# A hybrid decoder step on one core: products of the first norm ahead of the gates, state decay on another engine, row sums in a batch

## The chip, the cores and the metric

The kernel runs on one core of one Trainium2 chip. The metric is the device time in microseconds of one execution, the median of several runs; lower is better. In the profile the engines are PE (TensorE matmul), PEld (TensorE weight load), DVE (VectorE), ACT (ScalarE), POOL (GpSimd) and SP (SyncE, which issues the loads). `L782` is line 782 of the kernel that was profiled.

## The reference, cut to what matters

One decoder layer for 256 prompt tokens and 8 sample tokens (T = 264 columns in all), in float32, and a final norm. What the change touches is the start of the layer, up to the end of the DeltaNet branch, and the modulated norms:

```python
mod = c @ w_ada + b_ada                       # 6 vectors of 1024 per condition row
h = rmsnorm(x, norm_w) * (1 + sc) + sh        # three such norms: first, before the experts, final
qkv, z, b, a, ... = split(h @ w_in)
q, k, v = silu(short_conv(qkv))
q, k = l2norm(q) * DK ** -0.5, l2norm(k)      # 8 heads of 128 each
beta, g = sigmoid(b), -exp(A_log) * softplus(a + dt_bias)
# prompt: delta rule in chunks with a triangular solve per chunk and head
# samples: S = S * exp(g); vn = beta * (v - k S); S = S + k vn; o = q S
```

After it come the latent attention branch, the gates and the output projection, and a mixture of 32 experts (1024 by 2048 and 1024 by 1024 each). `S` are the samples' 64 states (8 heads by 8 samples) of 128 by 128 values.

## The kernel before, in words

Everything is laid out with features on the 128 partitions and tokens along the free axis. Each engine has its own hand-written program; their order is fixed by semaphores. SP streams 2 MB weight chunks in a fixed order through a ring of six slots, and refills a slot when TensorE has read the chunk in it. The stages, in order of time:

1. ACT squares x, TensorE sums the squares, and TensorE multiplies the four first chunks of `w_ada` with c (`modulate`, L731); ACT copies each result row (`mod_rows`, L1331), TensorE turns it (`turn_mod`, L737) and DVE adds the bias (`mod_bias`, L1610).
2. First norm. `norm_mod` on DVE forms 1 + scale (L1589), the reciprocal of the root (L1592) and eight products x times reciprocal (L1594), one for each of eight 128-row blocks; ACT applies scale and shift to the 256 prompt columns of each block (`modulate_prompt`, L1320); TensorE's `small_projection` (L761, L764) follows block by block.
3. The q/k/v projection: 24 output blocks m of 8 matmuls each (L782), with the short convolution on DVE and SiLU on ACT and DVE behind it. For the 16 q and k blocks ACT also squares the result (L1361, two buffers `sqb`), and TensorE sums the squares over the partitions with a four-column weight (L789): the result of block i goes to four rows at partition 32 * (i % 4) of bank 5.
4. Six more `w_ada` chunks (L731 again), then the roots and the spreading of the q/k norms over the partitions (`spread`, L813; DVE multiplies, L1661), the decays' sums (L823, L824), and copies of them in `cumc` (L1680).
5. For each of two chunks c of 128 tokens: gate rows by broadcast weights (L838 from `g_tok`, L841 from `beta_tok`), products of k with k and q (L847, L850), three more `w_ada` chunks, then the inverse of the triangular matrix by doubling in levels `lv` of 0 to 6. In each level DVE masks and updates (L1760, L1747, L1748), TensorE multiplies (L883), and ACT copies the first product (L1415, one for each of two groups g). L919 is the first matmul behind the inverse.
6. POOL, meanwhile, multiplies the samples' states, which SP loads in two 2 MB chunks (`SSM`), with their decays `egB` (L2009).
7. The samples' states, the attention branch, the gates, the output projection, the second norm, the router.
8. One pass for each of the 32 experts, whose 12.6 MB of weights go through the same ring.
9. The final norm: as stage 2, with the result stored by one DMA.

What decides the order inside a level is this code on ACT, which waits for TensorE's product of group g and copies it for TensorE's next product:

```python
for lv in range(1, LEVELS):
    for g in range(2):
        act.wait_ge(stage("lx_done"), (c * LEVELS + lv) * 2 + g + 1)
        if lv < LEVELS - 1:
            A(LTc[:, g, :], bank[g][:, 0:G2], ACT.Copy).then_inc(stage("lx_copied"), 1)
```

## Time and profile before

| what | value |
| --- | --- |
| three runs | 1711.02, 1712.14 (median), 1716.13 us |
| profiled execution, its own time | 1711.98 us |
| its span in the trace | 1710.1 us |
| PE busy / PEld busy | 1576.0 us (92%) / 850.6 us (50%) |
| DVE / ACT / POOL busy | 498.7 / 319.3 / 23.3 us |
| granted TensorE clock, mean | 0.967 of full speed |
| chain that ended last | PE 69%, DMA 14%, DVE 10%, issue 3%, ACT 2% |
| the four costliest lines in that chain | L508 14%, L551 13%, DMA of `biases` 13% (all experts), L1162 8% |

The span runs from the first to the last instruction of the program; 1.9 us of the device time lie outside it. A row of the timeline gives a group of equal instructions: start, duration from the first start to the last end, how many, and in brackets how long the engine had been idle before it and what it waited for. TensorE's float32 matmuls stand as two records each, so `x16` of L782 are eight matmuls. Bytes and GB/s are decimal; KB of a DMA are 1024 bytes.

### The profile page before, as it was taken

The numbers are of one execution on the slowest core, as the hardware profiler recorded it, in microseconds if no ns is written. First come the engines' busy times: TensorE is split into PE (matmuls) and PEld (weight loads), VectorE is DVE, ScalarE is ACT, GpSimd is POOL, SyncE is SP. The second block draws the span as 40 slices with busy tenths as digits, with TensorE's granted clock in tenths as the row PEclk, the third lists the DMA queues.
The fourth block names the chain that finished last, engine by engine and source line by source line (L and its number), as shares of the span: only waits on it lengthen the run. The fifth ranks groups of instructions, "written<-read, shape, count | busy, mean of one in ns | idle before, by whom it ended". The sixth has DMA issues, their size and how long they took to land.

```text
span 1710.1 us, 25650 instructions
## 1 busy us (share of the span) xinstructions
PE 1576.0 (92%) x10122; PEld 850.6 (50%) x10122; DVE 498.7 (29%) x1073; ACT 319.3 (19%) x688; POOL 23.3 (1%) x17
## 2 busy tenths in 40 slices
PE   5998687998879999789999999999999999999996
PEld 3777676576547768433333434333333334333332
DVE  1455765623210102422222222222222222222223
ACT  2222121112321110211111112111111112111113
POOL 0000300000000000000000000000000000000000
PEclk8998799999979999879999999999999999999999
DMA  9638502534238996249999999999999999999990
GB/s 403 272 110 333 208 30 121 209 124 164 72 105 304 346 343 264 94 190 405 428 427 425 428 427 427 429 428 428 429 429 427 427 423 428 420 428 423 429 420 34
DMA packets 59534, 541.25 MB, mean 317 GB/s; under 512 B 7218, under 2 KB 11442, under 8 KB 28626
## 3 DMA queue, kind: packets, MB, share of 16 engines
q1 hardware_dynamic: 58754, 534.65, 76.0%
q0 software_dynamic: 720, 5.76, 0.8%
q8 instruction: 43, 0.70, 0.2%
q14 instruction: 17, 0.14, 0.0%
HBM read 533.54 MB, written 6.84 MB: 316 GB/s over the span
## 4 chain that ended last, share of the span: by engine, by line
PE 69%; DMA 14%; DVE 10%; issue 3%; ACT 2%; SPq 1%; POOL 0%; DVEq 0%; ACTq 0%
PE banks L508 14%; PE banks L551 13%; DMA regC<-biases 13%; PE banks L1162 8%; PE banks L782 5%; PE banks L491 2%; PE banks L539 2%; DVE regA L629 2%; PE banks L521 2%; PE banks L1036 2%; PE banks L478 2%; PE banks L980 2%; DMA ring<-wpre 1%; DVE regA L627 1%; DVE regA L626 1%
## 5 line engine op out<-in xcount | busy, mean ns | idle before, releaser
L508 PE MATMUL banks<-ring,regA 128*64 128x512 f32 x2048 | 454.5, 596 | 0.8 <-ACT regA L566 0.8
L508 PEld LDWEIGHTS banks<-ring,regA 128*64 128x64 f32 x2048 | 144.7, 137 | 287.6 <-issue 287.6
L551 PE MATMUL banks<-ring,regC 128*64 128x512 f32 x1024 | 226.8, 595 | 0.0
L604 DVE TENSOR_TENSOR regB<-regB,banks 128x528 f32<-128x528 f32 x132 | 84.0, 699 | 383.7 <-PE banks L491 383.7
L551 PEld LDWEIGHTS banks<-ring,regC 128*64 128x64 f32 x1024 | 70.7, 137 | 131.8 <-issue 127.9
L624 DVE TENSOR_SCALAR regA<-banks 128x512 f32<-128x512 f32 x32 | 22.1, 691 | 339.4 <-PE banks L521 339.4
L569 ACT ACTIVATE regA<-regA 128x512 f32<-128x512 f32 x32 | 20.1, 630 | 517.3 <-DVE regA L624 517.3
L464 PE MATMUL banks<-regC,regA 128*64 128x512 f32 (+1 forms) x396 | 99.7, 621 | 3.3 <-DVE regA L596 3.3
L782 PE MATMUL banks<-hT,ring 128*128 128x264 f32 x384 | 90.3, 391 | 0.0
L782 PEld LDWEIGHTS banks<-hT,ring 128*128 128x128 f32 x384 | 71.5, 190 | 18.3 <-issue 7.0
L491 PE MATMUL banks<-regA,regC 64*128 64x264 f32 x528 | 73.8, 409 | 0.7 <-ACT regC L581 0.7
L491 PEld LDWEIGHTS banks<-regA,regC 64*128 64x128 f32 x528 | 45.4, 186 | 42.3 <-issue 26.0
L1162 PE MATMUL banks<-hT,ring 128*128 128x264 f32 x256 | 57.9, 387 | 0.0
L581 ACT ACTIVATE regC<-banks 128x512 f32<-128x512 f32 x32 | 19.1, 597 | 205.8 <-PE banks L551 205.8
L883 PE MATMUL banks<-regC 64*64 64x64 f32 x960 | 36.1, 235 | 19.8 <-DVE regC L1760 19.8
L1162 PEld LDWEIGHTS banks<-hT,ring 128*128 128x128 f32 x256 | 48.3, 190 | 10.0 <-issue 1.1
L539 PE MATMUL banks<-con_sb,regA 128*128 128x128 f32 x256 | 37.1, 288 | 17.3 <-DVE regA L629 17.3
L464 PEld LDWEIGHTS banks<-regC,regA 128*64 128x64 f32 (+1 forms) x396 | 22.8, 136 | 50.5 <-issue 50.5
L883 PEld LDWEIGHTS banks<-regC 64*64 64x64 f32 x960 | 33.4, 149 | 22.5 <-DVE regC L1760 22.5
L731 PE MATMUL banks<-ring,small_sb 128*32 128x128 f32 x1024 | 33.0, 282 | 9.4 <-DMA ring<-wpre 5.7
L569 ACT ACT_TABLE_LOAD x32 | 41.1, 1283 | 0.6
L539 PEld LDWEIGHTS banks<-con_sb,regA 128*128 128x128 f32 x256 | 31.0, 191 | 20.2 <-DVE regA L629 20.2
(445 smaller groups left out, 1646.6 us busy)
## 6 DMA issues: line engine op xcount, KB each, us to landing
ring<-w_gu SPq DMA_DIRECT2D x128, 2048.0 KB, 16.3
ring<-w_dn SPq DMA_DIRECT2D x64, 2048.0 KB, 13.9
ring<-wpre SPq DMA_DIRECT2D x41, 2048.0 KB, 13.7
ring<-kvT SPq DMA_DIRECT2D x64, 256.0 KB, 4.8
ring<-kv SPq DMA_DIRECT2D x64, 256.0 KB, 6.2
ring<-ssm SPq DMA_DIRECT2D x2, 2048.0 KB, 10.6
o_ssms<-ring POOLq DMA_DIRECT2D x2, 2048.0 KB, 7.4
con_sb<-con SPq DMA_DIRECT2D x1, 1269.0 KB
```

The lines of the kernel that those rows point to most:

```text
L464: mm = pe_mm(bank[2][SLOT * y:SLOT * (y + 1), :], lhsT=self_[r, i, :], rhs=h2tok[r, i, 4 * y:4 * y + 4, :].rearrange("p k c -> p (k c)"), ...
L478: mm = pe_mm(bank[3][:, P * q:P * (q + 1)], lhsT=gtok[:, P * q:P * (q + 1)], rhs=ident, start=True, stop=True)
L491: mm = pe_mm(bank[b + y][:, 0:T], lhsT=ytok[r, P * q:P * (q + 1)], rhs=selT[r, :], start=True, stop=True)
L508: mm = pe_mm(bank[x // 2][SLOT * (x % 2):SLOT * (x % 2 + 1), :], lhsT=hg[:, k % 4, SLOT * (k // 4):SLOT * (k // 4 + 1)], rhs=ring[c][:, 20 ...
L521: mm = pe_mm(bank[u][SLOT * y:SLOT * (y + 1), :], lhsT=ones[32 * u:32 * u + 1, 0:SLOT], rhs=brow[32 * u:32 * u + 1, HALF * y:HALF * (y + 1 ...
L539: mm = pe_mm(bank[4 - 2 * y][:, P * q:P * (q + 1)], lhsT=act_[:, P * q:P * (q + 1)], rhs=ident, start=True, stop=True)
L551: mm = pe_mm(bank[5][SLOT * y:SLOT * (y + 1), :], lhsT=actT[:, m % 4, SLOT * (m // 4):SLOT * (m // 4 + 1)], rhs=ring[c][:, D * (m % 4) + H ...
L569: A(sgm[:, :], gmn[:, :], ACT.Sigmoid, scale=1.702).then_inc(sig_ready, 1)
L604: V.tensor_tensor(pair, pair, banks[:, b:b + 2, 0:T], ALU.add).then_inc(acc_added, 1)
L782: mm = pe_mm(bank[m % 4][:, 0:T], lhsT=chunk_k(n, m % 4, k), rhs=hT[:, k, :], start=(k == 0), stop=(k == KD - 1))
L883: mm = pe_mm(out[rows, s], lhsT=left[rows, s], rhs=right(i, rows, cols), start=True, stop=True)
L1162: mm = pe_mm(bank[4 + m % 2][:, 0:T], lhsT=chunk_k(n, m % 4, k), rhs=rhs[:, k, :], start=(k == 0), stop=(k == KD - 1))
```

## The change

It has five parts.

- **First norm.** `norm_mod` is split in three. `normalised` (reciprocal and eight products) is now called ahead of the four `mod_bias` of the first chunks; `norm_scale` and `modulate_rest` come behind them. In all three norms ACT modulates the first five blocks (`ACT_K`), and DVE the other three with `tensor_scalar`.
- **Row sums.** The 16 row-sum matmuls of the q and k blocks leave the projection loop and are issued as one batch behind it. `sqb` grows from 2 buffers to 16 and moves to another place in the same memory.
- **Banks.** `spread` uses banks 0 to 3 in place of 4, 5, 0, 1.
- **Gate rows.** TensorE's wait for the last of the 16 q/k norms (`l2done`) moves from ahead of the gate rows of chunk 0 to behind them.
- **State decay.** POOL's two instructions over 128 x 4096 values are gone. ACT does the same in 64 instructions over 128 x 128 values with a per-partition scale, seven of them ahead of each level's copies: levels 3 to 6 of chunk 0 and 1 to 6 of chunk 1 (one in the last).

The diff (constants and buffers; TensorE; ACT; DVE; POOL):

```diff
@@ -43,10 +43,14 @@
 NJ1 = NJ + 1
 LEVELS = 7
 MOD_PRE = 10
-L2_BANKS = (4, 5, 0, 1)
+L2_BANKS = (0, 1, 2, 3)
 VALUE_BANKS = (2, 3, 0, 1)
 MOD_L2 = 7
 MOD_GDN = 3
+DECAY_FROM = 2
+DECAY_STEP = 7
+ACT_K = 5
+NORM_STEPS = 1 + 2 * KD - ACT_K
 
 
 C_ID, C_ONE, C_EPS = 0, 128, 256
@@ -156,7 +160,7 @@
 
         upad = cut(regC, 0, 3, 3 + NPR)
         sigb = cut(regC, 800, 2, T)
-        sqb = cut(regC, 1400, 2, T)
+        sqb = cut(regC, 3500, 2 * H, NPR)
         sq_s = cut(regC, 1400, 2 * H, NSA)
         rsb = cut(regC, 2900, 2, T)
         modA = cut(regC, 2300, KD, 9)
@@ -757,7 +761,10 @@
             def small_projection(out, weights_of, r):
 
                 for k in range(KD):
-                    pe.wait_ge(stage("modulated"), r * KD + k + 1)
+                    if k < ACT_K:
+                        pe.wait_ge(stage("modulated"), r * ACT_K + k + 1)
+                    else:
+                        pe.wait_ge(stage("normed"), r * NORM_STEPS + 1 + KD + k - ACT_K + 1)
                     pe_mm(out[:, 0:NPR], lhsT=weights_of(k), rhs=hT[:, k, 0:NPR], start=(k == 0), stop=(k == KD - 1), skip_group_check=True)
                 pe.wait_ge(h_ready, r + 1)
                 for k in range(KD):
@@ -783,13 +790,11 @@
                                start=(k == 0), stop=(k == KD - 1))
                 mm.then_inc(proj_ready, 1)
 
-                i = m - 3
-                if 0 <= i < 2 * H:
-                    pe.wait_ge(l2sq, i + 1)
-                    pe_mm(group_sum(i, slice(0, NPR)), lhsT=row_sum(i // 4, 4), rhs=sqb[:, i % 2, 0:NPR], start=(i < 4), stop=(i >= 2 * H - 4),
-                          skip_group_check=True).then_inc(l2ss, 1)
-
-
+            pe.wait_ge(l2sq, 2 * H)
+            for i in range(2 * H):
+                mm = pe_mm(group_sum(i, slice(0, NPR)), lhsT=row_sum(i // 4, 4), rhs=sqb[:, i, :], start=(i < 4), stop=(i >= 2 * H - 4),
+                           skip_group_check=True)
+            mm.then_inc(l2ss, 1)
             pe.wait_ge(proj_evac, CONVT)
             for i in range(4, MOD_PRE + 1):
                 if i < MOD_PRE:
@@ -815,8 +820,10 @@
 
             pe.wait_ge(stage("l2_rs"), 1)
             for i in range(2 * H):
+                if i == 0:
+                    pe.wait_ge(mod_row, MOD_PRE)
                 if i == 2:
-                    pe.wait_ge(mod_row, MOD_PRE)
+                    pe.wait_ge(mod_evac, MOD_PRE)
                 if i == 2 * H - 4:
                     pe.wait_ge(bg_done, 1)
                     for c in range(2):
...
@@ -825,7 +832,6 @@
                     pe.wait_ge(stage("bgm_ready"), 1)
                     pe_mm(bank[6][:, 96:160], lhsT=ones[0:NSA, :], rhs=bgm[0:NSA, :], start=True, stop=True).then_inc(once("cum_ready")[0], 1)
                 spread(i)
-            pe.wait_ge(l2done, 2 * H)
 
             for c in range(2):
                 tok = slice(c * P, (c + 1) * P)
@@ -842,6 +848,7 @@
                     if g == 0 and c == 0:
                         pe.wait_ge(*once("cum_read"))
                         pe.wait_ge(stage("egB_ready"), 1)
+                        pe.wait_ge(l2done, 2 * H)
                     for i in range(4):
                         h = 4 * g + i
...
@@ -1315,8 +1322,8 @@
 
             def modulate_prompt(r, out, sh, A9):
 
-                for k in range(KD):
-                    act.wait_ge(stage("normed"), r * KD + k + 1)
+                for k in range(ACT_K):
+                    act.wait_ge(stage("normed"), r * NORM_STEPS + 1 + (KD if r == 0 else k + 1))
                     A(out[:, k, 0:NPR], out[:, k, 0:NPR], ACT.Identity, scale=A9[:, k, 0:1], bias=mod[:, sh + k, 0:1]).then_inc(stage("modulated"), 1)
 
             def root(out, sums, scale):
@@ -1356,9 +1363,7 @@
                 i = m - 2
                 if 0 <= i < 2 * H:
                     act.wait_ge(silu_done, i + 1)
-                    if i >= 2:
-                        act.wait_ge(l2ss, i - 1)
-                    A(sqb[:, i % 2, 0:NPR], qkvT[:, i, 0:NPR], ACT.Square).then_inc(l2sq, 1)
+                    A(sqb[:, i, :], qkvT[:, i, 0:NPR], ACT.Square).then_inc(l2sq, 1)
             for i in range(4, 6):
                 mod_rows(i, i % 2)
             act.wait_ge(stage("conv_s"), 1)
@@ -1369,18 +1374,29 @@
             A(beta_tok[:, :, :], gsc[:, 0, :, :], ACT.Sigmoid).then_inc(ab_act, 1)
 
             act.wait_ge(silu_done, CONVT + 1)
-            act.wait_ge(l2ss, 2 * H)
             A(sq_s[:, :, :], qkvT[:, 0:2 * H, NPR:T], ACT.Square).then_inc(l2sq, 1)
             for i in range(6, MOD_PRE):
                 mod_rows(i, i % 2)
                 if i == MOD_L2:
-                    act.wait_ge(l2ss, 2 * H + 1)
+                    act.wait_ge(l2ss, 2)
                     A(rsb[:, 0, :], bank[5][:, 0:T], ACT.Sqrt, scale=1.0, bias=con[:, C_EPS:C_EPS + 1]).then_inc(root_ready, 1)
 
             link(A(gsc[:, 2, :, :], gsc[:, 1, :, :], ACT.Abs))
             link(A(gsc[:, 2, :, :], gsc[:, 2, :, :], ACT.Exp, scale=-1.0))
             link(A(gcol[:, 0, :], small[:, S_ALOG:S_ALOG + 8], ACT.Exp))
             A(gsc[:, 2, :, :], gsc[:, 2, :, :], ACT.Ln, bias=1.0).then_inc(ab_act, 1)
+
+            def decay(first):
+
+                for i in range(first, min(first + DECAY_STEP, H * NSA)):
+                    g, r = i // 32, i % 32
+                    if r == 0:
+                        act.wait_ge(stage("egB_ready"), 1)
+                        act.wait_ge(slot_in[(SSM + g) % RING], arrive[SSM + g])
+                    S = ssm_view[g][:, r // NSA, r % NSA, :]
+                    ins = A(S, S, ACT.Copy, scale=egB[:, i:i + 1])
+                    if r == 31:
+                        ins.then_inc(stage("decayed"), 1)
 
             for c in range(2):
 
@@ -1409,6 +1425,8 @@
                 for i in range(MOD_GDN):
                     mod_rows(MOD_PRE + MOD_GDN * c + i, 4 + i % 2)
                 for lv in range(1, LEVELS):
+                    if c == 1 or lv > DECAY_FROM:
+                        decay(DECAY_STEP * ((LEVELS - 1 - DECAY_FROM if c else 0) + lv - (1 if c else DECAY_FROM + 1)))
                     for g in range(2):
                         act.wait_ge(stage("lx_done"), (c * LEVELS + lv) * 2 + g + 1)
                         if lv < LEVELS - 1:
...
@@ -1584,20 +1602,34 @@
                 ins.then_inc(dve_line, 1)
                 dve.wait_ge(dve_line, line[0])
 
-            def norm_mod(r, x, out, sc, sh, nw, rs, A9):
-
-                link(V.scalar_tensor_tensor(A9, mod[:, sc:sc + KD, :], 1.0,
-                                            small[:, nw:nw + KD].unsqueeze(2).to_broadcast([P, KD, 9]), ALU.add, ALU.mult))
+            def normalised(r, x, out, rs):
+
                 dve.wait_ge(root_ready, (1, 6, 7)[r])
                 link(V.reciprocal(rs, rs))
                 for k in range(KD):
                     V.tensor_tensor(out[:, k, :], x[:, k, :], rs, ALU.mult).then_inc(stage("normed"), 1)
 
-                dve.wait_ge(stage("normed"), (r + 1) * KD)
+            def norm_scale(sc, nw, A9):
+
+                V.scalar_tensor_tensor(A9, mod[:, sc:sc + KD, :], 1.0, small[:, nw:nw + KD].unsqueeze(2).to_broadcast([P, KD, 9]),
+                                       ALU.add, ALU.mult).then_inc(stage("normed"), 1)
+
+            def modulate_rest(r, out, sh, A9):
+
+                dve.wait_ge(stage("normed"), r * NORM_STEPS + 1 + KD)
+                for k in range(ACT_K, KD):
+                    V.tensor_scalar(out[:, k, 0:NPR], out[:, k, 0:NPR], A9[:, k, 0:1], mod[:, sh + k, 0:1], ALU.mult, ALU.add).then_inc(stage("normed"), 1)
                 link(V.tensor_tensor(out[:, :, NPR:T], out[:, :, NPR:T], A9[:, :, 1:9], ALU.mult))
-                dve.wait_ge(stage("modulated"), (r + 1) * KD)
+                dve.wait_ge(stage("normed"), (r + 1) * NORM_STEPS)
+                dve.wait_ge(stage("modulated"), (r + 1) * ACT_K)
                 V.tensor_tensor(out[:, :, NPR:T], out[:, :, NPR:T], mod[:, sh:sh + KD, 1:9], ALU.add).then_inc(h_ready, 1)
                 dve.wait_ge(h_ready, r + 1)
+
+            def norm_mod(r, x, out, sc, sh, nw, rs, A9):
+
+                norm_scale(sc, nw, A9)
+                normalised(r, x, out, rs)
+                modulate_rest(r, out, sh, A9)
 
             dve.wait_ge(inputs_in, 48)
             link(V.memset(upad[:, :, 0:3], 0.0))
@@ -1610,11 +1642,13 @@
                 V.tensor_tensor(mod[:, 4 * i:4 * i + 4, :], bank[b][:, at:at + P].rearrange("p (m c) -> p m c", c=32)[:, :, 0:9],
                                 small[:, S_BADA + 4 * i:S_BADA + 4 * i + 4].unsqueeze(2).to_broadcast([P, 4, 9]),
                                 ALU.add).then_inc(mod_evac, 1)
+            dve.wait_ge(*once("upad_zero"))
+            normalised(0, xT[:, :, :], hT[:, :, :], rsb[:, 0, :])
             for i in range(4):
                 mod_bias(i, 2 + i % 2)
             dve.wait_ge(mod_evac, 4)
-            dve.wait_ge(*once("upad_zero"))
-            norm_mod(0, xT[:, :, :], hT[:, :, :], 8, 0, S_NMIX, rsb[:, 0, :], modA[:, :, :])
+            norm_scale(8, S_NMIX, modA[:, :, :])
+            modulate_rest(0, hT[:, :, :], 0, modA[:, :, :])
 
             dve.wait_ge(stage("rest_in"), 48)
             for m in range(CONVT + 1):
...
@@ -2002,11 +2036,6 @@
             pool.dma_start(t["o_convp"], convp[:, :, :]).then_inc(stored, 16)
             pool.dma_start(t["o_convs"], samp[:, :, :, :]).then_inc(stored, 16)
 
-            pool.wait_ge(stage("egB_ready"), 1)
-            for g in range(2):
-                pool.wait_ge(slot_in[(SSM + g) % RING], arrive[SSM + g])
-                S = ssm_view[g].rearrange("p h b v -> p (h b) v")
-                nc.gpsimd.tensor_tensor(S, S, egB[:, 32 * g:32 * g + 32].unsqueeze(2).to_broadcast([P, 32, P]), ALU.mult).then_inc(stage("decayed"), 1)
```

**TensorE, the projection loop (stage 3).** Before, the rows of the program from the small projection to the first later `w_ada` chunk. Names: `hT` is the normed input, `ring` a weight chunk, `regC` in L789 is `sqb`.

```order
L761 MATMUL banks<-hT,small_sb 16x256 x8
L764 MATMUL banks<-hT,small_sb 16x8 x8
L782 MATMUL banks<-hT,ring 128x264 x8
L775 MATMUL banks<-con_sb,regC 128x16 x2
L775 MATMUL banks<-con_sb,regC 8x16
L782 MATMUL banks<-hT,ring 128x264 x24
L789 MATMUL banks<-regC,con_sb 4x256
L782 MATMUL banks<-hT,ring 128x264 x8
...
L789 MATMUL banks<-regC,con_sb 4x256
L782 MATMUL banks<-hT,ring 128x264 x40
L731 MATMUL banks<-ring,small_sb 32x128 x64
```

And in the changed kernel (line numbers shift; L789 is now the projection, L795 the row sums):

```order
L768 MATMUL banks<-hT,small_sb 16x256 x8
L771 MATMUL banks<-hT,small_sb 16x8 x8
L789 MATMUL banks<-hT,ring 128x264 x8
L782 MATMUL banks<-con_sb,regC 128x16 x2
L782 MATMUL banks<-con_sb,regC 8x16
L789 MATMUL banks<-hT,ring 128x264 x184
L795 MATMUL banks<-regC,con_sb 4x256 x16
L735 MATMUL banks<-ring,small_sb 32x128 x64
```

The 16 row sums stood one behind each of the blocks 3 to 18; they now stand together behind block 23.

**DVE, the first norm (stage 2).** Before, from the last of the opening memsets to the first convolution:

```order
L1606 MEMSET banks 128x264
L1610 TENSOR_TENSOR mod<-banks,small_sb 128x36 x4
L1589 SCALAR_TENSOR_TENSOR regC<-mod,small_sb 128x72
L1592 RECIPROCAL regC<-regC 128x264
L1594 TENSOR_TENSOR hT<-xT_sb,regC 128x264 x8
L1597 TENSOR_TENSOR hT<-hT,regC 128x8x8
L1599 TENSOR_TENSOR hT<-hT,mod 128x8x8
```

In the changed kernel, the same stretch:

```order
L1638 MEMSET banks 128x264
L1608 RECIPROCAL regC<-regC 128x264
L1610 TENSOR_TENSOR hT<-xT_sb,regC 128x264 x8
L1642 TENSOR_TENSOR mod<-banks,small_sb 128x36 x4
L1614 SCALAR_TENSOR_TENSOR regC<-mod,small_sb 128x72
L1621 TENSOR_SCALAR hT<-hT,regC,mod 128x256 x3
L1622 TENSOR_TENSOR hT<-hT,regC 128x8x8
L1625 TENSOR_TENSOR hT<-hT,mod 128x8x8
```

The reciprocal and the products now stand ahead of the gates' bias, and three blocks of modulation (`TENSOR_SCALAR`) are new on DVE.

**ACT, the inverse of chunk 0 (stage 5).** Before, from the last exponential of the chunk's preparation to the output's copies:

```order
L1403 ACTIVATE regC<-regC 128x512
L1331 ACTIVATE mrow<-banks 128x128 x3
L1415 ACTIVATE regC<-banks 128x256 x10
L1417 ACTIVATE regC<-banks 64x256 x2
L1428 ACTIVATE regB<-banks 128x4x128 x2
```

In the changed kernel, behind the three copies of gate rows (L1397 is the decay, `ring` the states, L1433 and L1435 the levels' copies):

```order
L1433 ACTIVATE regC<-banks 128x256 x4
L1397 ACTIVATE ring<-ring,egB 128x128 x7
L1433 ACTIVATE regC<-banks 128x256 x2
L1397 ACTIVATE ring<-ring,egB 128x128 x7
L1433 ACTIVATE regC<-banks 128x256 x2
L1397 ACTIVATE ring<-ring,egB 128x128 x7
L1433 ACTIVATE regC<-banks 128x256 x2
L1397 ACTIVATE ring<-ring,egB 128x128 x7
L1435 ACTIVATE regC<-banks 64x256 x2
L1446 ACTIVATE regB<-banks 128x4x128 x2
```

Seven decay instructions stand ahead of the two copies of each level from the third on.

## Rows read from the trace of the kernel before

**Rows 1.** Busy time by stretch, expert stage: busy us (count) by engine, PEclk, DMA share, GB/s.
```profile
800.00:1000.00 200.00, 196.20 (x1049) 76.97 (x1046) 47.99 (x95) 32.69 (x53) 0.00 (x0) 1.00 1.01 427
```

**Rows 2.** Timeline, 10 to 45 us: start us, us, engine, line, operation, count [idle before].
```profile
15.38 0.48 ACT L1323 ACTIVATE regC<-banks,con_sb 128x264 f32<-128x264 f32 x1 [4.34 <-PE banks L717]
...
32.43 1.80 DVE L1592 RECIPROCAL regC<-regC 128x264 f32<-128x264 f32 x1
34.26 2.84 DVE L1594 TENSOR_TENSOR hT<-xT_sb,regC 128x264 f32<-128x264 f32 x8
34.73 4.04 ACT L1320 ACTIVATE hT<-hT,mod,regC 128x256 f32<-128x256 f32 x8 [3.44 <-DVE hT L1594]
...
35.38 6.16 PE L761 MATMUL banks<-hT,small_sb 128*16 128x256 f32 x16 [3.49 <-ACT hT L1320]
...
41.86 3.83 PE L782 MATMUL banks<-hT,ring 128*128 128x264 f32 x16
```

**Rows 3.** Chain that ended last, first microseconds: start us, us, what.
```profile
3.84 25.03 DMA ring<-wpre
```

**Rows 4.** DMA issues, 0 to 60 us: operation, count, KB each.
```profile
con_sb<-con SPq DMA_DIRECT2D x1, 1269.0 KB
...
regB<-convT SPq DMA_DIRECT2D x1, 384.0 KB
```

**Rows 5.** Busy time by stretch, 36 to 42 us, columns as in rows 1.
```profile
36.00:42.00 6.00, 6.00 (x32) 2.52 (x31) 1.55 (x6) 2.80 (x7) 0.00 (x0) 0.62 1.02 434
```

**Rows 6.** Timeline, end of the q/k/v projection.
```profile
117.23 3.83 PE L782 MATMUL banks<-hT,ring 128*128 128x264 f32 x16
...
121.51 18.07 PE L782 MATMUL banks<-hT,ring 128*128 128x264 f32 x80
...
140.19 3.70 PE L731 MATMUL banks<-ring,small_sb 128*32 128x128 f32 x128 [0.61 <-ACT regC L1349]
```

**Rows 7.** Timeline, 165 to 175 us: last q/k norms, then the gate rows.
```profile
168.31 1.82 DVE L1661 SCALAR_TENSOR_TENSOR regA<-regA,banks 128x264 f32<-128x264 f32 x4 [2.19 <-PE banks L813]
...
170.18 2.08 PE L838 MATMUL banks<-con_sb,g_tok 128*128 128x128 f32 x8 [1.98 <-DVE regA L1661]
...
171.01 0.19 DVE L1680 COPY cumc<-banks 128x32 f32<-128x32 f32 x1
...
173.72 1.05 PE L847 MATMUL banks<-regA 128*128 128x128 f32 x8
```

**Rows 8.** Timeline, first chunk's inverse, 195 to 232 us.
```profile
195.20 14.20 POOL L2009 TENSOR_TENSOR ring<-ring,egB 128x4096 f32<-128x4096 f32 x2 [46.91 <-DMA ring<-ssm]
...
197.90 0.42 DVE L1747 TENSOR_TENSOR regC<-regC,banks 128x256 f32<-128x256 f32 x1 [2.80 <-PE banks L883]
...
198.81 3.70 DVE L1760 TENSOR_TENSOR regC<-regC,con_sb 128x256 f32<-128x256 f32 x1
...
203.32 6.35 DVE L1760 TENSOR_TENSOR regC<-regC,con_sb 128x256 f32<-128x256 f32 x1
...
230.44 1.83 PE L919 MATMUL banks<-regC 128*128 128x128 f32 x14
```

**Rows 9.** All instructions of line 1760: ns min/median/max, first and last start.
```profile
L1760 DVE TENSOR_TENSOR regC<-regC,con_sb x24: 414/424/6352, 191.3 to 278.9; 128x256 f32<-128x256 f32 x24
```

**Rows 10.** Timeline, second chunk's inverse, 263 to 286 us.
```profile
263.86 0.42 DVE L1747 TENSOR_TENSOR regC<-regC,banks 128x256 f32<-128x256 f32 x1 [1.72 <-PE banks L883]
...
265.97 0.38 ACT L1415 ACTIVATE regC<-banks 128x256 f32<-128x256 f32 x1 [2.67 <-PE banks L883]
...
285.53 1.16 PE L919 MATMUL banks<-regC 128*128 128x128 f32 x8
```

**Rows 11.** ACT by line: names, shapes, count | busy us, mean ns | idle before us.
```profile
L1361 ACT ACTIVATE regC<-regA 128x256 f32<-128x256 f32 x16 | 6.8, 427 | 0.0
...
L1373 ACT ACTIVATE regC<-regA 128x128 f32<-128x128 f32 x1 | 0.3, 293 | 0.0
```

**Rows 12.** Timeline, last norm.
```profile
1705.47 0.23 DVE L1599 TENSOR_TENSOR regC<-regC,mod 128x64 f32<-128x64 f32 x1 [1.51 <-ACT regC L1320]
```

More of the change, by code:

```diff
@@ L1659, in _ @@
             for i in range(2 * H):
-                dve.wait_ge(l2ss, 2 * H + 2 + i)
+                dve.wait_ge(l2ss, 3 + i)
                 V.scalar_tensor_tensor(qkvT[:, i, :], qkvT[:, i, :], P ** -0.5 if i < H else 1.0, bank[L2_BANKS[i % 4]][:, 0:T], ALU.mult, ALU.mult).then_inc(l2done, 1)
```

## The prediction

> **What bounds the kernel now.** I read the chain that ended last first, then the expert stage by stretches, then the timeline of the first 300 us, where the change is. In the expert stage TensorE is busy 196.2 of 200 us and the DMA share is 1.01 at 427 GB/s [rows 1]: both are at their limit, and nothing of the change touches that stage. Its first loads are issued when TensorE releases ring slots, so it has no date of its own: whatever the start gains shifts it whole. The question is what the start gains. There TensorE waits for others, mostly DVE and ACT, so each part is read from the wait that ends last at its place.
>
> **First norm.** The root is ready at 15.86 us, while the last gate chunk lands only at 28.87 [rows 2, 3]. Before, the reciprocal (1.80) and the first product stand behind the gates: DVE starts them at 32.43, ACT follows at 34.73, TensorE at 35.38 [rows 2]. Moved ahead, reciprocal and products take 15.9 to 20.6, in the time of the weights' load; without that cover they would cost their 4.7 us again. ACT can then start at about 32.5, TensorE 0.65 later, as it does now, at 33.1: 2.3 us earlier. What is late next? The small projection takes 6.2 us, at a granted clock that stands at 0.62 over 36 to 42 us [rows 2, 5], so half clock most of that time, behind a TensorE idle of 3.49 us [rows 2]. With an idle of only 1.3 us it may keep the full clock. Then ACT's five blocks (4.04 / 8, 0.5 each) and DVE's three, which are done early, set the pace: done at about 37.2, 4.7 earlier. The next limit is the first projection chunk. Behind the last gate chunk (28.87) the queue still has 1269 KB and 384 KB [rows 4] and that chunk's 2 MB: 3.8 MB, at 434 GB/s [rows 5] 8.7 us, so it lands at 37.6 to 38, against a first use at 41.86 [rows 2]. Gain: 1.9 (clock half) to 3.9 (DMA bound); I take 3.6, since the shorter idle favours the full clock.
>
> **Row sums.** With a row sum behind it, one output block takes 121.51 - 117.23 = 4.28 us; the five without one take 18.07 together, 3.6 each, 3.56 without the tail [rows 6]. Sixteen times 0.72 is 11.5 us, and it includes TensorE's pauses around each. The loop's other engines have shown that they follow at 3.56 in those last blocks; ACT's squares go on, 0.43 each [rows 11]. The wait of 0.61 us for ACT's last copy behind the loop [rows 6] is covered by the batch. The batch itself is not in the trace. From the nearest row: the gate matmuls put four results in four groups of 32 output rows, as the row sums do; 64 matmuls of 128 columns take 3.70 us [rows 6], so 4096 columns take 1.85, and the batch has 16 x 256 = 4096. With 0.2 for the change of shape: 2.1. Upper bound, if they run one after the other as the projection's do: 3.56 / 8 x 256 / 264 = 0.43 each, 6.9. I take 2.1, because the output positions are those of the gate matmuls. Gain 11.5 + 0.6 - 2.1 = 10.0; 5.2 at the other end. The squares of the last q/k block are long there when the batch starts.
>
> The Trainium skill (TensorEngine Tiling (Array Packing), Key Properties and Theoretical Speedup) says that tiles work in parallel, up to four of them for a stationary operand of at most 32 columns, and that a change of tiling mode drains the engine. By it the batch would be 6.9 / 4 = 1.7 us, and the pauses around each row sum are such drains. No run here shows that of four-column weights yet.
>
> **Banks and gate rows.** Spreads into banks 2 and 3 now wait for the last gate bias on DVE. That is done before DVE's first two q/k norms, which need banks 0 and 1 only: nothing. The gate rows (L838, L841) used to start at 170.18, behind DVE's last norm; the products of k follow at 173.72 [rows 7], 3.54 us of TensorE. Moved ahead, they start when the last spreads are out, 168.3 [rows 7], and end at 171.85. The products also wait for the copy on DVE, done at 171.20 [rows 7], so about 171.35. Gain: 1.9, and 2.35 if the clock is full there; eight records of L838 took 2.08 against 1.05 of L847 [rows 7], so half clock. I take 1.9.
>
> **State decay.** POOL's two instructions run from 195.20 to 209.40. In just that time two of DVE's mask products (L1760, both inputs in the main memory) take 3.70 and 6.35 us [rows 8], against a median of 0.424 over 24 [rows 9], while L1747, which reads a bank, keeps its 0.42 [rows 8]. The second chunk runs the same levels with POOL idle, so it prices the whole: from L1747 of level 2 to L919 it takes 285.53 - 263.86 = 21.67 us, the first chunk 230.44 - 197.90 = 32.54 [rows 8, 10]. The difference, 10.87, is 9.2 of the two stalls and 1.7 of matmuls at a lower clock behind them. Bounds: 9.2, if the clock is low for another reason; 12, if levels 0 and 1 also run at full clock. I take 10.9.
>
> What ACT pays: 64 instructions, seven a level. In a level ACT waits 2.67 us for TensorE ahead of its first copy [rows 10]; the seven must fit in that gap. Price of one: the modulation, 256 columns with scale and bias from memory, steps at 4.04 / 8 = 0.505 [rows 2]; 128 columns fewer cost 0.427 - 0.293 = 0.134 less [rows 11]. So 0.37 at most, 7 x 0.37 = 2.6: hidden, barely. Below, 0.29 as the plain one of 128 columns [rows 11]; above, 0.505, which makes 3.5 and 0.9 us a level. The Trainium skill (ScalarE: Activation LUTs, What ACT_TABLE_LOAD costs) gives 186 ns + 0.833 ns a column and 93 ns for each operand from memory, with 93 of overlap: 0.29 a piece, 2.1 us for seven, by which half a microsecond of the gap is left. The first group needs the first state chunk; POOL's start shows that it landed at 195.20, while DVE enters level 2 only at 197.90, and the first decay stands behind that level's copies [rows 8]. I take no cost.
>
> **Last norms.** At the second norm TensorE's small projection sets the pace, not ACT: nothing. At the last, DVE's L1599 at 1705.47 waits for ACT's eighth block [rows 12]. Now ACT does five, and DVE puts three blocks in place of its wait of 1.51 us; at L1747's 0.42 [rows 8] they take 1.26: 0.25 us earlier, somewhat more with a scalar form. I take 0.3.
>
> **Sum.** 3.6 + 10.0 + 1.9 + 10.9 + 0.3 = 26.7 us. The profiled execution took 1711.98 us (1710.1 span and 1.9 around it), practically the median of 1712.14. 1711.98 - 26.7 = 1685.3 us.
>
> **Rivals.**
> - *The row sums do not run side by side* (four-column weights are handled as wide ones). Against: the same output groups as the gate matmuls. 4.8 us less: 1690.1.
> - *ACT is late in the levels.* Each decay costs 0.5 or the copies queue behind it. What stands behind a late decay is the level's first copy, and TensorE's doubling waits for that. For: the margin is thin by my own price. 0.9 x 9 levels = 8 us less: 1693.
> - *Slower than before.* Same mechanism, decisive when the decays of nine levels lose over 26.7 us, 3.0 a level: one decay of 0.81 us, (2.67 + 3.0) / 7, or 52 us of ACT in all. That is over twice the dearest price that I can derive. At 1.0 us a piece the time would be 1685.3 + 9 x 4.3 = 1724.
> - *No change.* The stalls of DVE are not POOL's doing and stay (10.9 less), and the experts' weight stream takes back the rest because its start isn't tied to the stages ahead. Against: L1760 is slow in POOL's time only, and the stream's slots are released by TensorE. 1712.
>
> **How the numbers follow.** Forecast as summed, each term within its bounds: 0.75. Row sums in series: 0.09. ACT late: 0.09. Slower: 0.02. Around no change: 0.02, and 0.03 for losses I have no name for, half of the gain or more. The best of all terms, 3.9 + 10.1 + 2.35 + 12 + 0.4, is 28.8, and full clock in the norms' stage, where those eight records cost double, may add 2 us: 1681. The other end holds the two middle rivals up to about 1692. Anything within 0.3% (5 us) is hardly told from no change; all cases but the last few lie far outside. Faster 0.95, same 0.03, slower 0.02.
>
> **What would show it.** Right: the small projection starts at about 33 us and the first projection block at about 38; all projection blocks 3.56 apart, the batch of 32 records about 2 us; the products of k start directly behind the gate rows; L1760's successor never over 0.5 us; seven decays in 2.1 to 2.6 us and TensorE's gaps in chunk 0 like those of chunk 1; the expert stage unchanged, only earlier. Wrong: a batch of 7 us, copies of a level starting after TensorE's product has long ended, TensorE waiting for a chunk at 33 to 40 us beyond 38, or a new pause of TensorE for its code or clock at 125 to 160 us.

## The result

The changed kernel takes 1703.04 us in the median of 15 runs (1683.51 to 1708.24); the kernel before, beside it, 1715.33 (1704.86 to 1732.34). The ratio is 0.9897, 95% interval 0.987 to 0.9923: faster by 1.0%. The forecast was 1685.3 with a range from 1681 to about 1692; its gain, 26.7 us, is more than twice the 12.3 us measured.

The median hides what the single times show. They lie in two groups with nothing between: six from 1683.5 to 1686.9 us, around the forecast, and nine from 1702.2 to 1708.2. The mean granted clock splits them too: 0.973 to 0.976 of full speed in the lower group, 0.961 to 0.965 in the upper. The profiled execution belongs to the lower group (1686.86 us). From its page:

```profile
span 1685.0 us, 25694 instructions
...
PE 1562.3 (93%) x10122; PEld 850.0 (50%) x10122; DVE 492.5 (29%) x1082; ACT 334.2 (20%) x743; POOL 9.0 (1%) x15
...
PEclk9998999999979999799999999999999999999998
```

Its timeline, first norm (start and duration in us, engine, line, operation, operands, shape, count, and in brackets the idle time before and what ended it):

```profile
32.26 2.58 ACT L1327 ACTIVATE hT<-hT,mod,regC 128x256 f32<-128x256 f32 x5 [1.14 <-DVE regC L1614]
...
32.92 3.87 PE L768 MATMUL banks<-hT,small_sb 128*16 128x256 f32 x16 [1.19 <-ACT hT L1327]
...
37.79 3.80 PE L789 MATMUL banks<-hT,ring 128*128 128x264 f32 x16 [0.61 <-DMA ring<-wpre]
```

TensorE starts the small projection 2.5 us earlier than in [rows 2], at full clock (3.87 us), and then waits for the first projection chunk: 4.07 us gained.

The same timeline at the projection's end, in the stage of the six `w_ada` chunks and in that of the gate rows:

```profile
123.84 1.91 PE L795 MATMUL banks<-regC,con_sb 128*4 128x256 f32 x32
125.57 3.45 PE L735 MATMUL banks<-ring,small_sb 128*32 128x128 f32 x118
130.94 0.60 PE L735 MATMUL banks<-ring,small_sb 128*32 128x128 f32 x10 [1.92 <-issue]
...
137.93 0.64 PE L735 MATMUL banks<-ring,small_sb 128*32 128x128 f32 x16 [2.22 <-issue]
...
144.69 1.73 PE L735 MATMUL banks<-ring,small_sb 128*32 128x128 f32 x54 [2.59 <-issue]
...
147.28 1.07 PE L818 MATMUL banks<-regC,con_sb 4*128 4x264 f32 x8
...
156.32 2.08 PE L844 MATMUL banks<-con_sb,g_tok 128*128 128x128 f32 x8
158.19 1.91 PE L847 MATMUL banks<-con_sb,beta_tok 128*128 128x128 f32 x8
159.90 1.40 PE L854 MATMUL banks<-regA 128*128 128x128 f32 x8
```

The kernel before, in the same stage:

```profile
148.85 0.64 PE L731 MATMUL banks<-ring,small_sb 128*32 128x128 f32 x16 [0.79 <-issue]
...
155.34 2.05 PE L731 MATMUL banks<-ring,small_sb 128*32 128x128 f32 x54 [2.32 <-issue]
...
158.54 1.26 PE L813 MATMUL banks<-regC,con_sb 4*128 4x264 f32 x8
```

The batch of row sums takes 1.91 us. The gate chunks start at 125.57 against 140.19 [rows 6], 14.62 earlier. In their stage TensorE now pauses three times with nothing to wait for ("issue"), 6.7 us in all; before it paused twice, 3.1 us. From the first gate chunk to the first spread it takes 21.71 us against 18.35, and from there to the gate rows 9.04 against 11.64. The products of k, which follow the gate rows directly, are 13.82 us earlier than in [rows 7].

And in the first chunk's inverse, with all instructions of the mask product (ns min/median/max) below:

```profile
183.35 0.42 DVE L1781 TENSOR_TENSOR regC<-regC,banks 128x256 f32<-128x256 f32 x1 [1.72 <-PE banks L890]
...
187.00 2.15 ACT L1397 ACTIVATE ring<-ring,egB 128x128 f32<-128x128 f32 x7
187.65 0.42 DVE L1781 TENSOR_TENSOR regC<-regC,banks 128x256 f32<-128x256 f32 x1 [1.72 <-PE banks L890]
...
205.04 3.63 PE L926 MATMUL banks<-regC 128*128 128x128 f32 x16
```

```profile
L1794 DVE TENSOR_TENSOR regC<-regC,con_sb x24: 416/426/426, 177.8 to 254.5; 128x256 f32<-128x256 f32 x24
```

From level 2 to the first matmul behind the inverse it is 205.04 - 183.35 = 21.69 us, against 32.54 in [rows 8] and 21.67 in [rows 10]. No mask product takes over 0.426 us; seven decays take 2.15 us and are done before DVE's update needs anything of ACT.

The span is 25.1 us shorter (1710.1 - 1685.0), 1.6 less than the sum. So in an execution of the lower group the change gains about what the prediction says. What puts most executions 17 us or more higher is the question of the experiments.

### The profile page after: what moved, and what is told of

The parts are those of the page before. It is cut to its first block and busy times, and to the rows that moved or that the text cites. A ratio compares the mean times of both kernels' runs of the same rounds, so it can differ in the third digit from the quotient of the medians.

```text
span 1685.0 us, 25694 instructions
## 1 busy us (share of the span) xinstructions
PE 1562.3 (93%) x10122; PEld 850.0 (50%) x10122; DVE 492.5 (29%) x1082; ACT 334.2 (20%) x743; POOL 9.0 (1%) x15
## 5 line engine op out<-in xcount | busy, mean ns | idle before, releaser
L789 PE MATMUL banks<-hT,ring 128*128 128x264 f32 x384 | 85.9, 386 | 0.6 <-DMA ring<-wpre 0.6
L789 PEld LDWEIGHTS banks<-hT,ring 128*128 128x128 f32 x384 | 72.8, 190 | 13.1 <-issue 0.7
L1169 PE MATMUL banks<-hT,ring 128*128 128x264 f32 x256 | 57.9, 387 | 0.0
L890 PE MATMUL banks<-regC 64*64 64x64 f32 x960 | 32.3, 220 | 11.7 <-DVE regC L1794 11.7
L525 PE MATMUL banks<-regC,con_sb 1*64 1x512 f32 x256 | 34.8, 612 | 3.9 <-DMA regC<-biases 3.9
## 6 DMA issues: line engine op xcount, KB each, us to landing
ring<-ssm SPq DMA_DIRECT2D x2, 2048.0 KB, 10.6
```

Source lines behind the costliest of these rows:

```text
L525: mm = pe_mm(bank[u][SLOT * y:SLOT * (y + 1), :], lhsT=ones[32 * u:32 * u + 1, 0:SLOT], rhs=brow[32 * u:32 * u + 1, HALF * y:HALF * (y + 1 ...
L789: mm = pe_mm(bank[m % 4][:, 0:T], lhsT=chunk_k(n, m % 4, k), rhs=hT[:, k, :], start=(k == 0), stop=(k == KD - 1))
L890: mm = pe_mm(out[rows, s], lhsT=left[rows, s], rhs=right(i, rows, cols), start=True, stop=True)
L1169: mm = pe_mm(bank[4 + m % 2][:, 0:T], lhsT=chunk_k(n, m % 4, k), rhs=rhs[:, k, :], start=(k == 0), stop=(k == KD - 1))
```

## The experiments

Each experiment ran beside the kernel before on the same chip. A kernel's times fell into two groups, called the lower and the upper level, whose medians lie 15 to 21 us apart (26 in e7, which has a single run on the upper one), unless one of the groups was empty. The kernel before has them too, but in all its 102 timed runs only 10 lie on the upper one (1727.6 to 1733.7 us; the other 92 from 1704.9 to 1720.0). Which level a run belongs to is told by its time; a profile on the upper level was taken in e8, e11 and e12, of the whole change none.

### One part at a time, and the change without one part

**The whole change again** (e1).

> The changed kernel once more, to see its two levels of time (span 1681 to 1685 at a mean granted clock of .973 to .976, and 1700 to 1706 at .961 to .965) and, if the profiled execution falls on the upper one, to find the stretch in which it lies. Theory A (a place in the program that the change moved is left at half clock longer in some executions): both levels appear again, in about 6 executions of 15 the lower, and the kernel before, on the same chip, shows one level about 1711 to 1717. Theory B (the levels belong to the chip or the moment and touch any kernel): the kernel before shows two levels 17 us apart as well, on the same chip.

Six runs: 1684.78, 1685.65, 1688.93 and 1703.26, 1705.04, 1705.57. Two levels again, 12 of 21 executions on the upper one with the first 15.

**Single parts**: POOL's instructions replaced by ACT's `decay` (e2), the row sums in one batch (e3), the first norm split (e4), each in the kernel before.

> The kernel before with the states' decay on ACT alone. The sum of the prediction gives 10.9 us (9.2 to 12), a time of about 1701 in the profiled execution. Theory A: if this part is what brings the second level, its times split 17 us apart; otherwise they stay together. Theory B: splits as every other kernel on this chip does.

> The kernel before with the q/k row sums in one batch behind the projection alone. By the prediction 10.0 us less (11.9 for what goes away from the projection's end and the rope's wait, less 2.1 for the batch), about 1702; 5.2 us of batch if the column groups ran in series, about 1705. Theory A: if this part brings the second level, its times split 17 us apart.

> The kernel before with the first norm's products split off and made during the loads, alone. By the prediction 3.6 us less (1.9 to 3.9), about 1708. Theory A: if this part brings the second level, its times split 17 us apart.

On the lower level their medians are 1701.2 (9 of 12 runs), 1704.7 (11 of 12) and 1707.2 (10 of 12), against 1713.5 for the kernel before (27 of 29). The parts can also be read from the start of the first outer product of the samples' states, behind all four: 307.72 us before, 297.13, 298.27 and 303.57 with one part, 283.33 with the whole change. That is 10.6 for the decay (sum: 10.9), 9.5 for the row sums (10.0), 4.2 for the norm (3.6), 24.4 for all (26.4 without the last norm). Each is one profile, and they scatter: in e1 the same program has that start at 286.18, 2.9 us later, with more time at half clock and pauses of 5.1 in place of 6.7 us ahead of it. So these sums are good to about 3 us. All three have the upper level, in 3, 1 and 2 of 12: no single part makes it frequent.

**Without one part** (e5 to e8).

> The whole change without its row sums in a batch. On the lower level the sum gives 1684.7 + 10.0 = 1695 us. So far single parts lie on the upper level (17 to 21 us higher) in 1 to 3 executions of 12, the kernel before in about 4 of 44, the whole change in 12 of 21. Theory A (one part of the change, or where it moves a later stretch, makes the upper level frequent): the four kernels that leave out one part each differ in their share of the upper level, and the one that lacks the guilty part falls back to 1 or 2 in 10. Theory B (no part, only the moment on the chip): all four and the kernel before show like shares. A profile of an execution on the upper level will show the stretch: by the mean granted clocks (.974 against .962) about 38 us more at the lower clock, where TensorE sets the pace.

> The whole change without the states' decay on ACT. Lower level: 1684.7 + 10.9 = 1696 us. Theory A: if the decay is the guilty part, the upper level (about 1713) comes in 1 or 2 executions of 10 here, and in half of those of the other three. Theory B: like shares.

> The whole change without the first norm's split. Lower level: 1684.7 + 3.6 = 1688 us. Theory A: if the first norm is the guilty part, the upper level (about 1706) is rare here. Theory B: like shares.

> The whole change without the gate rows and banks ahead of the last norms. Lower level: 1684.7 + 1.9 = 1687 us. Theory A: if this part is guilty, the upper level (about 1704) is rare here. Theory B: like shares.

| without | lower level | upper level |
| --- | --- | --- |
| row sums | 6 runs, 1690.6 to 1693.3 | 4 runs, 1710.7 to 1715.7 |
| decay | 7 runs, 1690.9 to 1704.6 | 3 runs, 1716.6 to 1721.7 |
| first norm | 3 runs, 1689.2 to 1689.8 | 1 run, 1715.2 |
| gate rows | 5 runs, 1687.6 to 1695.6 | 5 runs, 1706.0 to 1709.8 |

The lower levels' medians are 1691.7, 1699.7, 1689.4 and 1691.2 us, against 1695, 1696, 1688 and 1687 expected; the run without the decay spreads over 14 us. No kernel falls back to 1 or 2 in 10, so the shares name no guilty part. But the profile of the one without the gate rows was taken on the upper level (span 1704.7 us). Its windows (engine busy times, granted clock PEclk, DMA share, GB/s):

```profile
280.00:290.00 10.00, 8.15 (x46) 4.95 (x39) 8.67 (x11) 2.06 (x3) 0.00 (x0) 0.83 0.00 2
290.00:300.00 10.00, 10.00 (x21) 3.72 (x19) 2.81 (x4) 0.00 (x0) 0.00 (x0) 0.50 0.01 2
300.00:310.00 10.00, 10.00 (x20) 4.38 (x20) 3.63 (x3) 0.39 (x1) 0.54 (x1) 0.50 0.50 210
310.00:320.00 10.00, 10.00 (x29) 3.87 (x32) 3.06 (x4) 0.39 (x1) 0.53 (x1) 0.50 0.12 52
320.00:330.00 10.00, 10.00 (x58) 6.16 (x51) 6.36 (x5) 0.39 (x1) 0.00 (x0) 0.96 1.01 391
```

The whole change on the lower level, the same stretch:

```profile
280.00:290.00 10.00, 8.14 (x33) 4.12 (x33) 8.31 (x12) 0.39 (x1) 0.00 (x0) 1.00 0.00 0
290.00:300.00 10.00, 10.00 (x39) 4.50 (x38) 6.06 (x8) 0.39 (x1) 0.54 (x1) 1.00 0.50 211
300.00:310.00 10.00, 10.00 (x60) 5.72 (x59) 6.30 (x7) 0.78 (x2) 0.53 (x1) 1.00 0.82 311
```

Here is the 17 us: TensorE is at half clock (1.2 GHz) from about 287 to 321 us, 34 us, although it is busy 10.00 of 10. Its work there takes about twice as long, and TensorE sets the pace. Over 1700 us such a stretch lowers the mean clock by 0.010, about what parts the two groups of the result. The timelines at its entry, first without the gate rows, then the whole change:

```profile
280.41 3.83 PE L985 MATMUL banks<-hT,ring 128*128 128x264 f32 x16
286.09 1.63 PE L998 MATMUL banks<-regC 32*128 32x512 f32 x4 [1.85 <-DVE regC L1831]
287.65 2.13 PE L985 MATMUL banks<-hT,ring 128*128 128x264 f32 x4
289.71 2.08 PE L998 MATMUL banks<-regC 32*128 32x512 f32 x4
```

```profile
277.65 3.83 PE L987 MATMUL banks<-hT,ring 128*128 128x264 f32 x16
283.33 1.13 PE L1000 MATMUL banks<-regC 32*128 32x512 f32 x4 [1.86 <-DVE regC L1833]
284.39 1.16 PE L987 MATMUL banks<-hT,ring 128*128 128x264 f32 x4
```

The work and the idle ahead of it are the same, 1.85 and 1.86 us, and so in each profile with the idle unfilled, before the change too (1.85 to 1.88): TensorE has done the z block and waits for DVE's `vnm`, then alternates outer products, which use 32 of the 128 rows (L998 or L1000), with steps of the next z block. Only the clock differs. The theory from here on: where that idle falls between the moments at which the clock can change decides, and the change, which moves the idle by 24.4 us (21.5 in e1), has moved it to an unlucky place (theory P).

### Shifting the idle, and filling it

The pad, in the whole change or in the kernel before, behind the second chunk's inverse:

```diff
+                for k in range(3 if c == 1 else 0):        # or 6
+                    pe_mm(bank[0][:, 0:T], lhsT=ident, rhs=hT[:, k, :], start=True, stop=True)
                 for g in range(2):
                     pe.wait_ge(stage("x_done"), (c + 1) * 2 * LEVELS if g == 1 else (c + 1) * 2 * LEVELS - 1)
```

The fill, in the idle itself (`beta` moves from bank 6 to unused columns of bank 4):

```diff
             project_z(0, 0, KD)
+            for k in range(3):
+                pe_mm(bank[6][:, 0:T], lhsT=chunk_k(ZZ, 0, k), rhs=hT[:, k, :], start=True, stop=True)
             pe.wait_ge(*once("krow_copied"))
```

> The changed kernel, plus six matmul records of 264 columns into an unused bank (1.4 us, results thrown away) in TensorE's idle of 1.86 us ahead of the first outer product of the samples' states; the copy of beta moves to bank 4 for it. Theory P (in some executions that idle ends just before the clock is reviewed, TensorE then works 34 us at half clock through the samples' states, and that is the upper level): the upper level vanishes, all executions at about 1685 to 1690. Theory D (the decay on ACT brings the upper level by itself, or it lies elsewhere): the upper level stays in about half of the executions, median about 1700.

> The changed kernel, plus 1.44 us of idle work (three products of 264 columns into bank 0) behind the second chunk's inverse, about 20 us ahead of that idle; the idle itself stays. Theory P with a phase that the program's own length sets: the idle falls 1.4 us later against the clock's moments, as it does in the kernel before; the upper level is seen in about 1 of 10 executions, so the median is about 1687, below the changed kernel's 1700 although there is more work. Theory P with a random phase: the share stays about half. Theory D: the share stays about half, every time 1.4 us longer.

> The kernel before with the same 1.44 us of idle work at the same place. Theory P with a phase set by the program's length: here the shift leads into the bad place; the upper level comes in more than half of the executions, median about 1730 against 1713. Theory P with a random phase, and theory D: about 1 in 10 as before, median 1714.5.

> The changed kernel with six such products, 2.87 us. [...] Theory P with a random phase, and theory D: about half, median anywhere from 1688 to 1705, lower level 1687.

The next four kernels keep the unlucky shift and take the idle away, or fill it with the kernel's own work: with `beta` in bank 4 the second z block needn't wait for DVE any more.

```diff
             project_z(0, 0, KD)
+            project_z(1, 0, 3)
+            cuts = ((3, 5, 6, 7, 8), (0, 2, 4, 6, 8))
...
-                    project_z(1 + g, 2 * x, 2 * x + 2)
+                    project_z(1 + g, cuts[g][x], cuts[g][x + 1])
```

> The changed kernel with three of the eight steps of the second z block made in the idle ahead of the first outer product (1.44 us of its own work, no more idle work), the other five between the outer products. Theory P: no upper level; the work moved into the idle also shortens the stretch by up to 1.4 us: about 1683 to 1686 in all executions. Rival (the thin products behind the idle let the clock fall): with fewer dense steps between them the upper level stays or becomes frequent, about 1700.

> The kernel that lay on the upper level in all its executions (six products of idle work, median 1704.8), with the idle filled by thrown-away products. Theory P: all executions back on the lower level, 1685.9 + 2.9 = about 1688.5. Rival (thin products): stays at 1704.

> The kernel before with three pad products (median 1729.3, all on the upper level), with the idle filled. Theory P: back to about 1713. Rival: stays at 1729.

> The six pad products with the idle filled by the second z block's own steps. Theory P: 1704.8 falls to about 1687, all executions together. Rival: some executions stay 17 us higher, since fewer dense steps lie between the thin products.

| kernel | median us | runs on the upper level | ratio to before, 95% |
| --- | --- | --- | --- |
| before | 1711.1 to 1715.3 | 10 of 102 | 1 |
| before, shifted 1.4 us (e11) | 1729.3 | 6 of 6 | 1.0104 (1.0082 to 1.0126) |
| the same, idle filled (e15) | 1714.5 | 0 of 12 | 1.0003 (0.9976 to 1.0029) |
| whole change | 1703.0, 1696.1 | 12 of 21 | 0.9897 (0.987 to 0.9923) |
| shifted 1.4 us (e10) | 1688.35 | 1 of 6 | 0.9877 (0.9839 to 0.9915) |
| shifted 2.9 us (e12) | 1704.8 | 10 of 10 | 0.9959 (0.9942 to 0.9976) |
| the same, idle filled (e14) | 1691.7 | 0 of 6 | 0.9878 (0.9841 to 0.9915) |
| the same, own work in the idle (e16) | 1689.7 | 0 of 6 | 0.9858 (0.9822 to 0.9895) |
| whole change, idle filled (e9) | 1685.94 | 0 of 5 | 0.9843 (0.982 to 0.9866) |
| whole change, own work in the idle (e13) | 1684.96 | 0 of 6 | 0.9839 (0.9803 to 0.9875) |

The same pad costs the kernel before 18 us and gains the changed one 8 to 15; twice the pad puts the changed kernel wholly on the upper level. A random phase, or a level that belongs to the decay, would have left the shares alone. One run of six in e10 alone would not tell that from a half; the six of six and ten of ten do. The filled kernels come back to the lower level in all of 35 executions, e14 and e16 3 us above what was expected. The clock of the kernel before with the pad (e11), by windows:

```profile
300.00:310.00 10.00, 7.75 (x84) 4.69 (x76) 9.69 (x11) 2.06 (x3) 0.58 (x1) 1.00 0.13 52
310.00:320.00 10.00, 9.92 (x23) 4.36 (x24) 5.31 (x7) 0.00 (x0) 0.00 (x0) 0.59 0.01 2
320.00:330.00 10.00, 10.00 (x22) 3.86 (x20) 2.69 (x3) 0.39 (x1) 0.55 (x1) 0.50 0.50 210
330.00:340.00 10.00, 10.00 (x21) 4.25 (x20) 3.76 (x4) 0.00 (x0) 0.00 (x0) 0.50 0.00 0
```

It is the stretch of e8 again, in a kernel that holds nothing of the change. The entry in e12, and in e14, which differs from it in the fill alone:

```profile
282.25 3.83 PE L989 MATMUL banks<-hT,ring 128*128 128x264 f32 x16
287.95 1.13 PE L1002 MATMUL banks<-regC 32*128 32x512 f32 x4 [1.87 <-DVE regC L1835]
289.01 2.04 PE L989 MATMUL banks<-hT,ring 128*128 128x264 f32 x4
290.98 2.07 PE L1002 MATMUL banks<-regC 32*128 32x512 f32 x4
```

```profile
280.50 3.83 PE L989 MATMUL banks<-hT,ring 128*128 128x264 f32 x16
284.16 1.50 PE L1007 MATMUL banks<-hT,ring 128*128 128x264 f32 x6
286.18 1.13 PE L1002 MATMUL banks<-regC 32*128 32x512 f32 x4 [0.52 <-DVE regC L1837]
287.24 1.16 PE L989 MATMUL banks<-hT,ring 128*128 128x264 f32 x4
288.33 1.13 PE L1002 MATMUL banks<-regC 32*128 32x512 f32 x4
```

In the first the clock falls 1.2 us behind the idle's end. In the second the idle is 0.52 us and the same outer products keep the full clock. So the idle lets the clock fall, not the thin products alone; that they are part of what keeps it down is likely but was not taken apart. (The fill comes with `beta` in bank 4; that move alone was not run.)

The traces also date the clock's changes. In all thirteen profiles with the idle unfilled a half-clock stretch ends in the first chunk's inverse or just behind it, 69 to 94 us ahead of the z block (in e1 one more short stretch follows, at 238 to 242 us). The row of the changed kernel with that rise, then two of e1:

```profile
208.00:209.00 1.00, 1.00 (x9) 1.00 (x9) 0.29 (x1) 0.00 (x0) 0.00 (x0) 0.80 0.00 0
...
210.00:211.00 1.00, 1.00 (x7) 1.00 (x6) 0.69 (x1) 0.00 (x0) 0.00 (x0) 0.50 0.00 0
211.00:212.00 1.00, 1.00 (x11) 1.00 (x11) 0.00 (x0) 0.00 (x0) 0.00 (x0) 1.00 0.00 0
```

| profile | that rise, us | start of the z block ahead of the idle | distance | clock falls behind the idle's end |
| --- | --- | --- | --- | --- |
| whole change | 208.4 | 277.65 | 69.3 | no |
| whole change (e1) | 211.0 | 280.50 | 69.5 | no |
| without gate rows (e8) | 211.5 | 280.41 | 68.9 | 0.5 us |
| before with the decay alone (e2) | 222.2 | 291.45 | 69.3 | no |
| shifted 1.4 us (e10) | 207.8 | 278.31 | 70.5 | no |
| shifted 2.9 us (e12) | 210.6 | 282.25 | 71.6 | 1.2 us |
| before | 214.6 | 302.02 | 87.4 | no |
| before, shifted 1.4 us (e11) | 216.3 | 304.40 | 88.1 | 1.8 us |

Counted from the program's start the same program's z block moves by 2.9 us from one execution to the next, twice the pad. Counted from the rise it stays within 0.6 us where the program behind the rise is the same (the first four rows), and the pads move it on (70.5 and 71.6; 88.1 against 87.4 is within the scatter). The rest agree: e3, e4 and e6, which have the inverse of the kernel before, lie at 87.2, 86.5 and 87.0, and e5 and e7, whose rise comes earlier in the inverse, at 93.3 and 93.4, all without a fall. So it is not the program's length from its start that sets the place: the half-clock stretches ahead of it line the program up with the clock's moments. And the whole change seems to stand at an edge, 69.3 and 69.5 without a fall, 68.9 in e8 with one, which would fit its 12 of 21; these are three profiles only. e13 shows the repair with no idle work:

```profile
278.15 5.16 PE L985 MATMUL banks<-hT,ring 128*128 128x264 f32 x22
283.83 1.13 PE L998 MATMUL banks<-regC 32*128 32x512 f32 x4 [0.51 <-DVE regC L1833]
284.88 1.16 PE L985 MATMUL banks<-hT,ring 128*128 128x264 f32 x4
```

It has the lowest median: all six runs lie between 1684.18 and 1687.61 us. It is hardly faster than the lower level of the change (1683.5 to 1688.9); the 1.4 us that I gave as the best case didn't come. What it gains is that the upper level is gone.

## Why the prediction was wrong

- **First norm**, 3.6: 4.07 at the first projection block, and 4.2 alone in e4. Mechanism as told: full clock in the small projection (3.87 us), and the first chunk as next limit (37.79, forecast 37.6 to 38). The lower bound of 1.9 has no working; a start 2.3 us earlier at half clock gives 2.3.
- **Row sums**, 10.0: in the changed kernel 14.62 - 4.07 = 10.55, alone 9.5. The batch takes 1.91 us (taken 2.1, upper bound 6.9), so the four groups run side by side; the rival of a batch in series is out. The estimate by the Trainium skill (TensorEngine Tiling (Array Packing), Theoretical Speedup) was 1.7, and the trace is near that.
- **Banks and gate rows**, 1.9: the gate rows stand ahead as told, TensorE's idle of 1.98 us ahead of them is gone, and the stretch from the first spread to them is 2.60 us shorter. But the products of k are only 13.82 us earlier, 0.80 less than the gate chunks: the `w_ada` stage ahead is 3.36 us longer, since TensorE's pauses in it grew from 3.1 to 6.7 us. The prediction had named "a new pause of TensorE for its code or clock at 125 to 160 us" as a sign that it would be wrong and had given it no price. The pauses go with the batch of row sums: 3.2 us in e2 and e4, which lack it, 4.9 in e3 and 5.1 in e1, which have it. What they are, the profile calls "issue" and no run took apart.
- **State decay**, 10.9: 32.54 - 21.69 = 10.85, and 10.6 in e2. The seven decays take 2.15 us of the gap of 2.67 and are hidden; ACT is not late. The estimate by the Trainium skill (ScalarE: Activation LUTs, What ACT_TABLE_LOAD costs) was 2.1, nearer than my own 2.6. The two long mask products are gone with POOL's instructions: the longest is 0.427 us in e2, which changes nothing else, and 6.348 in e6, which puts POOL's instructions back. That settles that POOL caused them. The Trainium skill (SBUF — State Buffer, Who interferes with whom) says that a DVE instruction with two inputs in the main memory contends with a GpSimd instruction that reads it; the 3.70 and 6.35 us that turned into 0.426 agree.
- **Last norm**, 0.3: not resolved; nothing in the span speaks against it.
- **Sum**: 26.7 us, against 25.1 in the span of the profiled execution, and 1683.5 to 1688.9 us in all nine executions on the lower level (forecast 1685.3). That the forecast lies in the middle of them is in part luck: its base, 1711.98, is 3 us under the median of the 15 runs beside the change.
- **Two slips in the rivals**, without effect here: a decay of 0.81 us is 1.6 times the dearest price of 0.505, not over twice; and "ACT is late" gives 1693, which lies outside the range that was to hold it.

**The step that failed** is the first one: "whatever the start gains shifts it whole", and with it the sum made against one profiled execution. Between the change and the expert stage lie other stages, and I put what the shift costs them at nothing: I took for granted that a stage whose instructions and waits are unchanged keeps its time when it starts earlier. In the samples' states it doesn't. There TensorE stands 1.86 us idle ahead of thin products, and the kernel before, by its times, kept the full clock there in nine executions of ten. Shifted by 21 to 24 us it loses it in 12 of 21, and then pays 17 us or more (34 us at half clock in e8). The median of 15 runs fell on that side by nine to six; with two runs more on the lower level it would have lain in the range, so the miss of the number hangs on a share near one half, the missing term does not. I had looked at the clock only where the change was. Of the rivals, none was this: "slower" and "no change" were worked out as losses of the change's own parts, and the 0.03 for losses without a name held it. So the range's upper end, about 1692, covered the lower level and nothing else.

What stays open: why the earlier half-clock stretches bring the program into nearly the same place against the clock's moments each time; the table of dates shows that they do. No profile shows the whole change itself on the upper level; that its stretch is the one of e8 rests on its times, its mean clock and the fills. Also open is the rest of the scatter on one level, 5 us in the whole change, but 10 in e14, 13 in e15, 14 in e6 and 15 in the kernel before; profiles of one kernel differ in the length of other half-clock stretches, and e15's longest is outside the samples' states.

## What to carry to other kernels

When a change moves unchanged work in time, look in the trace for each place behind it where TensorE idles one or two microseconds between thinly filled matmuls, and count a possible half-clock stretch there as a rival, with a price (here 17 us); a single profile at full clock doesn't prove that the place is safe. Read the single times, not only the median: two groups with nothing between are two courses of the program, and a pad of one or two microseconds ahead of the suspected place tells quickly whether its position decides. The cure is to fill the idle, best with work that only waited for a bank.

## What the runs showed of the hardware

- TensorE can stay at 1.2 GHz for 34 us while it is busy all the time (10.00 of 10 us, granted clock 0.50), with alternating outer products on 32 rows and 128-row steps, and run the same sequence at 2.4 GHz throughout in another execution. Being busy didn't raise the clock; it rose behind about 320 us in e8, where the outer products are over.
- The moments at which it changes are not random against a late part of the program. The share of unlucky executions went from 10 in 102 to 6 in 6, and from 12 in 21 to 1 in 6 and 10 in 10, with shifts of 1.4 and 2.9 us; a random place would have left it alone. The Trainium skill (TensorE: Matmul & The Clock Gate, What's actually happening) calls the window in which activity is watched free-running and variable from run to run. Counted from the program's start the traces agree (the rise at 208.4 and 211.0 us in two executions of one program); counted from that rise the program keeps its place within 0.6 us.
- Four-column weights on four output groups run side by side: 32 records of 256 columns in 1.91 us, where one after the other, at the price of the projection's matmuls, would make 6.9 (an estimate).
